# Output stage of a hybrid decoder layer: the first tile's convolution half in steps of one head, weights in four loads

## Reference, cut to what matters

```python
def group_rmsnorm(x, g, n_groups):
    shp = x.shape
    xf = x.astype(jnp.float32).reshape(shp[:-1] + (n_groups, shp[-1] // n_groups))
    y = xf * lax.rsqrt(jnp.mean(xf * xf, axis=-1, keepdims=True) + EPS)
    return (y.reshape(shp) * g.astype(jnp.float32)).astype(x.dtype)
...
    o = group_rmsnorm(o, norm_g, HGRN_HEADS) * jax.nn.silu(g_out.astype(jnp.float32))
...
    return group_rmsnorm(b_gate * y, norm_g, CONV_GROUPS)
...
        h = h + jnp.concatenate([y_hgrn, y_conv], axis=-1) @ w_out[l]
        h = h + moe_ffn(rmsnorm(h, norm_ffn_g[l]), w_router[l], router_bias[l],
```

## Time and profile before

| | us |
|---|---|
| timed runs | 1641.84, 1641.07, 1640.34; median 1641.07 |
| the profiled execution, its own time | 1643.35 |
| its span | 1641.8 |
| TensorE busy (matmul) | 1557.7 (95%) |
| VectorE, ScalarE, GpSimd busy | 759.8, 653.5, 668.0 (46%, 40%, 41%) |
| output stage | about 438 to 700 |
| expert loop and end | about 705 to 1642 |

### The profile page before, as it was taken

One profiled execution on the slowest core, in us unless ns is written; L12 is line 12 of the kernel. 1 busy time (PEld: TensorE's weight loads), 2 busy tenths in 40 slices (PEclk: granted clock), 3 DMA queues, 4 the chain that ended last, 5 costly groups with the idle time before them and its releaser, 6 DMA issues.

```text
span 1641.8 us, 30075 instructions
## 1 busy us (share of the span) xinstructions
PE 1557.7 (95%) x10204; PEld 1340.5 (82%) x10204; DVE 759.8 (46%) x1536; ACT 653.5 (40%) x1054; POOL 668.0 (41%) x825
## 2 busy tenths in 40 slices
PE   6999999999799999889999999999999999999990
PEld 5789989989545666679999999999999999999980
DVE  4333778788678864323333333333333333333332
ACT  6434544434443221024444444444444444444443
POOL 0422336063203322325545554545554545555541
PEclk9999999999899999989999999999999999999995
DMA  5389221121240113369999999999999999999977
GB/s 181 98 293 314 110 78 60 68 77 52 107 194 15 48 44 124 108 231 320 314 335 322 320 331 322 316 329 320 328 323 323 323 325 326 319 325 332 315 234 237
DMA packets 100745, 375.17 MB, mean 229 GB/s; under 512 B 14960, under 2 KB 31921, under 8 KB 79711
## 3 DMA queue, kind: packets, MB, share of 16 engines
q1 hardware_dynamic: 60622, 246.60, 41.5%
q0 software_dynamic: 40080, 128.04, 28.8%
HBM read 300.68 MB, written 73.91 MB: 228 GB/s over the span
## 4 chain that ended last, share of the span: by engine, by line
PE 54%; DMA 1%; DVE 1%; issue 0%; ACT 0%; POOL 0%; POOLq 0%; ACTq 0%; DVEq 0%; SPq 0%
PE gu L1741 35%; PE ype L1763 4%; PE yrest L1752 4%; PE ype L1764 4%; PE xp L1722 4%; PE ype L1765 3%; PE xp L1729 1%; DMA acc_rows<-YE,sia 1%; DVE A L1928 1%; DMA A<-acc_rows 0%; POOL acc_rows L1659 0%; DVE rtf L1926 0%; ACT XS L1821 0%; ACT XS L1817 0%; ACT YF L1832 0%
## 5 line engine op out<-in xcount | busy, mean ns | idle before, releaser
L1741 PE MATMUL gu<-XS,place 128*128 128x160 f32 x4160 | 587.8, 300 | 0.7 <-ACT XS L1821 0.7
L1741 PEld LDWEIGHTS gu<-XS,place 128*128 128x128 f32 x4160 | 575.2, 190 | 6.2 <-ACT XS L1821 1.1
L1891 DVE TENSOR_TENSOR WL<-place,WH 128x2048 fp32r<-128x2048 f32 x65 | 149.0, 2293 | 315.5 <-ACT WH L1813 315.5
L1659 POOL DMA_INDIRECT acc_rows<-YF,sib x65 | 104.3, 1605 | 217.9 <-issue 171.1
L1826 ACT ACTIVATE SS<-gu 128x160 f32<-128x160 f32 x130 | 39.4, 303 | 364.9 <-PE gu L1741 364.9
L1896 DVE TENSOR_TENSOR SS<-SS,gu 128x160 f32<-128x160 f32 x130 | 41.3, 317 | 261.6 <-ACT SS L1826 261.6
L1645 POOL COPY gta<-tables 128x1 f32 (+1 forms) x65 | 138.3, 2128 | 9.5 <-POOLq L982 9.5
L1127 POOL DMA_INDIRECT slot_table<-pay,si x64 | 63.1, 986 | 174.4 <-DVEq L1426 157.3
L1836 ACT ACTIVATE YE<-ype,gta 128x512 f32<-128x512 f32 x130 | 89.5, 688 | 109.7 <-PE ype L1765 109.7
L1813 ACT ACTIVATE WH<-place 128x2048 fp32r<-128x2048 f32 x65 | 123.5, 1900 | 0.7 <-issue 0.7
L1663 POOL DMA_INDIRECT acc_rows<-YE,sia x65 | 103.3, 1589 | 30.7 <-issue 22.4
(11 more groups left out here) (311 smaller groups left out, 2804.1 us busy)
## 6 DMA issues: line engine op xcount, KB each, us to landing
place<-in_w_gate_e SPq DMA_DIRECT2D x65, 1024.0 KB
place<-in_w_up_e SPq DMA_DIRECT2D x65, 1024.0 KB
place<-in_w_down_e SPq DMA_DIRECT2D x65, 1024.0 KB
place<-in_w_in POOLq DMA_DIRECT2D x16, 512.0 KB, 7.0
late_parts<-wq_parts POOLq DMA_DIRECT2D x8, 1024.0 KB, 6.1
late_parts<-xn_parts POOLq DMA_DIRECT2D x8, 1024.0 KB, 5.8
wf_parts<-late_parts POOLq DMA_DIRECT2D x8, 1024.0 KB, 4.9
w_low<-late_parts POOLq DMA_DIRECT2D x8, 1024.0 KB, 4.9
```

The source lines that it names most:

```text
L1659: pool.indirect_dma_start(acc_q, bass.IndirectOffsetOnAxis(ap=si[q][1][:, :], axis=0), YF[q][:, :], None, compute_op=ALU.add).then_inc(s_a ...
L1741: last = pe.matmul(gu[f][:, k, :], raw[:, t, f * P:f * P + P], XS[:, q, t, :], start=(t == 0), stop=(t == KT - 1))
L1891: tt(WL[q][:, :], WR[q][2][:, :], WH[q][:, :].bitcast(F32), ALU.subtract).then_inc(s_dlo, 1)
```

## The change

For the first tile alone the convolution half goes ahead of the gated half on every engine, with signals of its own. ScalarE squares the convolution half first and signals each half; TensorE makes the means of the convolution half, then of the gated half, each with a signal; ScalarE's root of each half has its own wait and signal; VectorE takes the reciprocal and the multiply head by head, each head signalled; TensorE multiplies each head with both column halves of `wo` as it comes (`first_conv`), before `means(1)`. `wo` is loaded in four pieces (convolution rows, columns 0 to 511 and 512 to 1023, then the gated rows), each with a semaphore. The counts of `s_y`, `s_rt`, `s_ms` and `s_sq` that the later tiles wait for are raised to match.

```diff
-            for k in range(2):
-                sp.dma_start(wo[:, :, 512 * k:512 * k + 512], w_out[:, :, 512 * k:512 * k + 512]).then_inc(s_wo[k], 16)
+            for part, rows in enumerate((slice(HEADS, 2 * HEADS), slice(0, HEADS))):
+                for k in range(2):
+                    cols = slice(512 * k, 512 * k + 512)
+                    sp.dma_start(wo[:, rows, cols], w_out[:, rows, cols]).then_inc(s_wo[part][k], 16)
...
+            def first_means():
+
+                for n, k in enumerate((1, 0)):
+                    pe.wait_ge(s_sq, n + 1)
+                    pe.matmul(ms[k][:, :, :].rearrange("p h t -> p (h t)"), K.ones[:, :],
+                              R[0][:, HEADS * k:HEADS * k + HEADS, :].rearrange("p h t -> p (h t)"), start=True, stop=True) \
+                        .then_inc(s_ms, 1)
+
+            def first_conv():
+
+                for h in range(HEADS):
+                    pe.wait_ge(s_y, h + 1)
+                    for half in range(2):
+                        if h == 0:
+                            pe.wait_ge(s_wo[0][half], 16)
+                        pe.matmul(op[half][:, :], YC[:, h, 0:P], wo[:, HEADS + h, 512 * half:512 * half + 512],
+                                  start=(h == 0), stop=False)
...
             def project(j, half, part):
-                pe.wait_ge(s_y, 2 * j + part + 1)
+                pe.wait_ge(s_y, 2 * j + part + HEADS)
                 if part == 0:
-                    if j:
-                        pe.wait_ge(s_h2, 2 * (j - 1) + half + 1)
-                    else:
-                        pe.wait_ge(s_wo[half], 16)
+                    pe.wait_ge(s_h2, 2 * (j - 1) + half + 1)
+                elif j == 0:
+                    pe.wait_ge(s_wo[1][half], 16)
...
-            means(0)
+            first_means()
             for j in range(TT):
-                if j not in SOON:
+                if j == 0:
+                    first_conv()
+                    means(1)
+                elif j not in SOON:
                     project(j, 0, 0)
-                if j == 0:
-                    means(1)
-                    project(j, 1, 0)
                 project(j, 0, 1)
...
+            def first_squares():
+                act.activation(R[0][:, HEADS:2 * HEADS, :], YC[:, :, 0:P], ACT.Square).then_inc(s_sq, 1)
+                act.activation(R[0][:, 0:HEADS, :], K.QO[:, :, 0:P], ACT.Square).then_inc(s_sq, 1)
+
+            def first_root(n):
+                k = 1 - n
+                act.wait_ge(s_ms, n + 1)
+                act.activation(R[0][:, HEADS * k:HEADS * k + HEADS, :], ms[k][:, :, :], ACT.Sqrt,
+                               bias=K.eps[:, 0:1], scale=1.0 / P).then_inc(s_rt, 1)
...
-            squares(0)
-            roots(0)
+            first_squares()
+            first_root(0)
+            first_root(1)
             gate_sigmoid(0)
             gate_sigmoid(1)
             squares(1)
...
+                if j == 0:
+                    dve.wait_ge(s_rt, 1)
+                    for h in range(HEADS):
+                        step(nc.vector.reciprocal(conv[:, h, :], conv[:, h, :]))
+                        stt(YC[:, h, cols], YC[:, h, cols], K.ng[:, 1, h:h + 1], conv[:, h, :], ALU.mult, ALU.mult).then_inc(s_y, 1)
+                    dve.wait_ge(s_rt, 2)
+                else:
+                    dve.wait_ge(s_rt, j + 2)
+                    step(nc.vector.reciprocal(conv, conv))
+                    for h in range(HEADS):
+                        last = stt(YC[:, h, cols], YC[:, h, cols], K.ng[:, 1, h:h + 1], conv[:, h, :], ALU.mult, ALU.mult)
+                    last.then_inc(s_y, 1)
                 step(nc.vector.reciprocal(gated, gated))
```

More of the change, by code:

```diff
@@ L1034, in phase_out_route @@
         s_w, s_ws = sem("router_in"), sem("shared_in")
-        s_wo, s_c = [sem(f"wo_in{i}") for i in range(2)], sem("gffn_in")
+        s_wo, s_c = [[sem(f"wo_{n}_in{i}") for i in range(2)] for n in ("conv", "gated")], sem("gffn_in")
         s_h = [sem(f"h_in{i}") for i in range(NH)]
@@ L1145, in _ @@
             done = {"turn": 0, "down": 0}
+            def first_means():
[12 more added lines that the diff above has]
+                                  start=(h == 0), stop=False)
             def means(j):
-                pe.wait_ge(s_sq, j + 1)
-                if j:
-                    pe.wait_ge(s_rt, j)
+                pe.wait_ge(s_sq, j + 2)
+                pe.wait_ge(s_rt, j + 1)
                 for k in range(2):
@@ L1281, in _ @@
         def _(act):
+            def first_squares():
[6 more added lines that the diff above has]
+                               bias=K.eps[:, 0:1], scale=1.0 / P).then_inc(s_rt, 1)
             def squares(j):
                 if j >= 2:
-                    act.wait_ge(s_y, 2 * j - 2)
+                    act.wait_ge(s_y, 2 * j - 3 + HEADS)
                 act.activation(R[j % 2][:, 0:HEADS, :], K.QO[:, :, j * P:j * P + P], ACT.Square)
@@ L1288, in roots @@
             def roots(j):
-                act.wait_ge(s_ms, j + 1)
+                act.wait_ge(s_ms, j + 2)
                 for k in range(2):
@@ L1355, in mix @@
             def mix(j):
-                dve.wait_ge(s_rt, j + 1)
                 r, cols = R[j % 2], slice(j * P, j * P + P)
                 conv, gated = r[:, HEADS:2 * HEADS, :], r[:, 0:HEADS, :]
[L1360 to L1363, removed]
+                if j == 0:
[10 more added lines that the diff above has]
+                    last.then_inc(s_y, 1)
                 step(nc.vector.reciprocal(gated, gated))
```

## The result

The changed kernel takes 1644.72 us (median), the kernel before 1641.05; the ratio is 1.0023 with a 95% interval of 1.0017 to 1.0029. It is slower, by 2.8 to 4.8 us, where 1640.3 us, 0.75 us faster, had been forecast and the range ended at 1642.8. The profiled execution took 1644.55 us with a span of 1643.0.

The account below looks back on a forecast made before the run. Ahead of the expert loop, VectorE was taken to set the pace once tile 1's means are done: 2.5 us sooner, less one TensorE clock fall of 1.75 us, gives 0.75 us gained, 1640.3 us; range 1638.0 to 1642.8.

Parts of the forecast that it names:

- loads without a price: Output matrix in four loads: two extra issues on SP delay nothing needed; gated pieces also arrive in time; cost nothing.
- VectorE free of tile 0: VectorE finishes tile 0's gated half and six memsets at 453.65, before tile 1 is ready for it.
- the clock's second place: TensorE's 3.9 us rest ahead of tile 1's projection: clock falls with chance three in four, costing 1.75 us (0 to 2.1).
- (a): Rival: TensorE's clock falls in neither place, so the full 2.5 us is gained, 1638.6 us; chance 0.11.
- (c): Rival: first weight pieces land much faster, so VectorE's own tile 0 work is the limit; 4.6 us gained, 1636.5; chance 0.04.
- The sum: Means of tile 1 2.5 us sooner, less one clock fall of 1.75 us: 0.75 us gained, 1640.3 us.
- (b): Rival: TensorE's clock falls in both places, 2.5 - 3.5 = -1.0 us, 1642.1 (1642.8 at 2.1 each); chance 0.35.
- the first place: TensorE's rests around tile 0's first projection matmuls: clock falls with chance one in two, costing 1.75 us (0 to 2.1).

Follow-up runs that it names:

- after_3: The changed kernel unaltered, profiled a third time; span 1642.6 us, stretch from the stage's start to the last tile's transposes 209.61 us.
- after_4: The changed kernel unaltered, profiled a fourth time; span 1643.4 us, stretch from the stage's start to the last tile's transposes 210.07 us.
- order_alone: Kernel before, with tile 0's second column half of the convolution projection moved ahead of the means of tile 1; 1649.92 us against 1641.98, ratio 1.0041.
- fill_first: Changed kernel plus short unread matmuls of constants behind the first means and between the first head's column halves; 1643.58 us against 1641.98 before, ratio 1.0007.
- means_between: Changed kernel with the means of tile 1 placed between the two column halves of tile 0's convolution projection; 1636.29 us against 1640.88 before, ratio 0.9978.
- fill_second: Changed kernel plus unread matmuls in TensorE's rest ahead of tile 1's first projection; 1640.55 us, ratio to before 1.0002; changed kernel beside it 1643.90.

## Why the prediction was wrong

The steps up to TensorE's first matmul were right: heads at about 1.25 us (reciprocals at 442.31 and each 1.26 us after, 0.95 us each), first projection at 444.25 (443.9 forecast), the rest of it at 446.87 behind the second piece (446.5), loads without a price, VectorE free of tile 0 at 453.9 (453.65). The rest ahead of tile 1's projection was 3.98 us (3.9), and its fall fed through VectorE's wait in full, as the section on the clock's second place said. The rivals (a), no fall, and (c), no wait for weights, did not occur.

Two steps failed.

**One fall taken as likeliest where both are the rule.** The sum took the full clock for the 14 convolution matmuls or for tile 1's first projection, one of the two. In all four traces of the changed kernel both ran slow, so that the case that came was (b), given 0.35. The step behind it is the clock at which tile 0's projection starts: the prediction took it to stand at 1.00 after the first means, as it "stood just then in the trace of before", and gave one in two to a fall from there. That premise came in two traces of four (after_3, after_4), and there the clock fell during the pair of matmuls or as it ended; in the other two it had fallen during the first means and not come back. The rest ahead of the pair was also longer than the 0.9 us of the prediction: the means no longer ran at the half clock throughout (2.44 us for four instead of 3.63), ended at 442.26 and left TensorE idle for 1.99 us, and for 2.46 us in after_3 and after_4. Why the clock falls 1.4 us into the means in one execution and more than 4 us later in another, behind the same rest of 2.35 us, no run shows.

**The price of a fall.** The sum took 1.75 us each, with 2.1 as the upper end. Measured: 2.3 us for the first (8.54 against 6.28 with it filled) and 2.8 us for the second (wait 4.30 against 1.49; 4.28, 4.33 and 4.50 in the others; 2.5 in order_alone and fill_first). Both rows I took it from understate it. The four means of the earlier trace rows ran slow from their first to their last, and their 1.75 us is only what fits into four matmuls. The projection of the earlier trace rows, 2.1 us dearer, began when the clock had already been half for part of its rest (1.00 to 446.0, 0.54 from 450.4 in the earlier trace rows), so part of the slow time cost nothing. In the changed kernel the fall at 468.6 came 1.1 us before work resumed, and 5.6 us of the slow 6.7 fell on matmuls. The price is half of the slow time that falls on matmuls: 5.6 us gave 2.8, 4.9 us in order_alone gave 2.5, and 4.5 us in the first place (446.9 to 451.4) gave 2.3.

With these prices the sum is 2.5 - 2.3 - 2.8 = -2.6 us, and the stretch says 206.9 - 209.7 = -2.7 us. The upper end of the range, worked out with 2.1 for each, could not hold that. It had also been given none of the spread of the runs, where the lower end had half of it (0.75 us, which leads to 1637.8 and not to the 1638.0 put down); with as much at the top, 1643.5 would still have been short. And (b) needed not twice its price to lose 3.3 us: 5.8 us in place of 3.5 is 1.7 times, and the measured 5.1 us are 1.5 times. The advice of the Trainium skill, TensorE: Matmul & The Clock Gate, section "HAM oscillation — how this bites in real kernels", against waits of this size between groups of matmuls is what this case's traces show: in six executions with a rest of 3.98 or 3.99 us ahead of tile 1's projection the clock fell six times.

**What stays open.** 2.7 us are accounted for; the medians are 3.7 us apart over all runs, 3.0 on the chip of the second comparison, and the interval begins at 2.8. The traced executions do not hold the rest: the mean spans of the four of each kernel are 2.6 us apart, of which 2.1 us stand at the start of the expert loop (703.5 against 705.6 in the mean). Four of the 20 timed runs of the changed kernel took 1647.6 to 1648.6 us, where the slowest of the kernel before took 1642.8, and no trace is of such an execution. The varying part from the logits of tile 7 to the row of experts (25.7 to 30.8 us over all traces, with TensorE's idle time put down to issue) adds to single executions of both kernels. Whether it does so more often in the changed one, four traces of each can't tell, and no run separated it.

## What to carry to other kernels

Feeding an engine sooner is worth only what reaches the next engine that sets the pace. Here that was VectorE, which waited for the means of the next tile, and the change put 16 matmul instructions ahead of them where 8 had been. Put what the pacing engine waits for first, and keep the rest of the work as filler behind it: the same pieces in another order went from 2.7 us slower to 4.8 us faster in this stage. When an order is changed, look for new rests of TensorE of several microseconds, and price one by how much of the slow time falls on matmuls, not by a row in which the slow work ended by itself or had rested through part of it.

## What the runs showed of the hardware

Matmuls whose result nobody reads, 3.6 us of them, made the kernel 3.4 us faster by the medians (1640.55 against 1643.90), since they kept TensorE's clock at 1.00. A rest of 1.96 us inside busy work left the clock up (means_between); rests of 3.98 or 3.99 us lost it in all six executions that had one, for 2.5 to 3.0 us.

The rest alone did not decide when the clock fell. Behind a rest of 2.34 or 2.35 us it fell 1.3 to 1.4 us into the means in two executions of the changed kernel, and in the two others, as in fill_second and fill_first, these means ran at 1.00 throughout.

In the first trace the clock, half from 441.2 on, stayed so through rests of 1.99 and 0.57 us with a pair of matmuls between them and for 4.5 us of the work that followed. In after_3 and after_4 it was up through a rest of 2.46 us and fell with the pair. In the one trace with 1.5 us of short matmuls of constants behind the pair and 1.05 us behind the means (fill_first), it stayed at 1.00.
